# Ones behind the second mixer's values, and five short stretches in another order, in a two-block transformer on one core

## What is computed

```
x = x + gt1 * merge(attention(h), gla(h));  x = x + gt2 * square(relu(h2 @ w1)) @ w2     # first block
h = h + mlstm(rmsnorm(h))                                                                # second mixer
h = h + square(relu(rmsnorm(h) @ w1)) @ w2
h = h + sigmoid(rmsnorm(h) @ gate_w + b) * (p @ ple_w)
return rmsnorm(h) * norm_final
```

```
num = s @ v            # 256 values a head
den = sum of s over the keys
h   = num / max(abs(den), exp(-m))
```

## Time and profile before

| | us |
|---|---|
| median of 3 runs | 924.65 (924.34 to 925.21) |
| profiled execution | 924.22 |
| its span | 922.4 |
| PE busy | 896.7 (97%) |
| PE weight loads busy | 766.2 (83%) |
| DVE busy | 624.5 (68%) |
| ACT busy | 478.7 (52%) |
| POOL busy | 10.0 (1%) |

### The profile page before, as it was taken

The page is one execution under the profiler, slowest core; times in us unless marked ns, Lnnn a source line. Parts: engine busy times, 40 slices in busy tenths (PEclk is TensorE's granted clock), DMA queues, the critical chain, the costliest instruction groups (busy, mean ns, idle before and its releaser), DMA issues.

```text
span 922.4 us, 14154 instructions
## 1 busy us (share of the span) xinstructions
PE 896.7 (97%) x5144; PEld 766.2 (83%) x5144; DVE 624.5 (68%) x990; ACT 478.7 (52%) x759; POOL 10.0 (1%) x21
## 2 busy tenths in 40 slices
PE   7999999999999999999999999999999999999995
PEld 2788888887788887889999998897888999999984
DVE  2668779879688878765555557766767855555577
ACT  3647545565565575465444444444645744444453
POOL 0200000000000000000000000000000000000000
PEclk9999999999999999999999999999999999999998
DMA  9955212326346877646555558254334665555521
GB/s 360 340 180 178 70 52 86 114 92 200 114 143 227 255 245 246 218 141 210 183 183 182 182 185 270 94 183 141 131 114 159 224 223 198 196 191 193 188 91 46
DMA packets 45376, 162.10 MB, mean 176 GB/s; under 512 B 5616, under 2 KB 5760, under 8 KB 45329
## 3 DMA queue, kind: packets, MB, share of 16 engines
q1 hardware_dynamic: 42896, 155.73, 50.0%
q0 software_dynamic: 1296, 4.02, 1.6%
q10 hardware_dynamic: 1136, 1.70, 0.5%
HBM read 160.39 MB, written 1.05 MB: 175 GB/s over the span
## 4 chain that ended last, share of the span: by engine, by line
PE 82%; DVE 9%; ACT 4%; DMA 3%; issue 2%; SPq 0%; DVEq 0%; ACTq 0%
PE bank L685 68%; DVE w_lo L1657 3%; DMA arena<-in_early 2%; PE bank L857 2%; PE bank L940 1%; PE bank L1137 1%; ACT w_hi L1233 1%; PE bank L847 1%; DMA raw<-in_stream 1%; PE bank L960 1%; PE bank L955 1%; PE bank L1166 1%; PE bank L864 1%; PE bank L805 1%; DVE act_lo L1657 1%
## 5 line engine op out<-in xcount | busy, mean ns | idle before, releaser
L1657 DVE TENSOR_TENSOR w_lo<-raw,w_hi 128x1024 fp32r<-128x1024 f32 x244 | 288.1, 1220 | 161.8 <-ACT w_hi L1233 161.5
L1233 ACT ACTIVATE w_hi<-raw 128x1024 fp32r<-128x1024 f32 x244 | 245.0, 1051 | 195.1 <-PE bank L685 165.4
L685 PE MATMUL bank<-w_hi,act_lo 128*128 128x512 f32 x720 | 293.0, 407 | 0.1
L685 PE MATMUL bank<-w_lo,act_hi 128*128 128x512 f32 x720 | 281.3, 391 | 0.0
L685 PE MATMUL bank<-w_hi,act_hi 128*128 128x512 f32 x720 | 280.8, 390 | 0.0
L685 PE MATMUL bank<-act_lo,w_hi 128*128 128x256 f32 x640 | 183.0, 286 | 3.6 <-DVE act_lo L1657 2.5
L685 PE MATMUL bank<-act_hi,w_hi 128*128 128x256 f32 x640 | 181.1, 283 | 0.0
L685 PE MATMUL bank<-act_hi,w_lo 128*128 128x256 f32 x640 | 181.0, 283 | 0.0
L685 PEld LDWEIGHTS bank<-w_lo,act_hi 128*128 128x128 f32 x720 | 135.1, 188 | 29.3
L685 PEld LDWEIGHTS bank<-w_hi,act_lo 128*128 128x128 f32 x720 | 135.5, 188 | 26.7 <-issue 1.7
L685 PEld LDWEIGHTS bank<-w_hi,act_hi 128*128 128x128 f32 x720 | 135.6, 188 | 26.2 <-issue 1.4
(11 more groups left out here) (250 smaller groups left out, 782.9 us busy)
## 6 DMA issues: line engine op xcount, KB each, us to landing
raw<-in_stream SPq DMA_DIRECT2D x278, 512.0 KB, 4.5
arena<-in_early SPq DMA_DIRECT2D x14, 512.0 KB, 12.0
res<-in_x ACTq DMA_DIRECT2D x1, 1024.0 KB, 8.9
raw<-in_early SPq DMA_DIRECT2D x2, 512.0 KB, 13.6
arena<-in_ctx SPq DMA_DIRECT2D x1, 1024.0 KB, 13.5
res<-in_x POOLq DMA_DIRECT2D x1, 1024.0 KB, 7.7
arena<-in_norm_final POOLq DMA_DIRECT2D x1, 512.0 KB, 4.4
arena<-in_ple_b POOLq DMA_DIRECT2D x1, 512.0 KB, 5.4
```

What stands on the lines that cost most here:

```text
L685: last = pe.matmul(o, left, right, start=start and m == 0, stop=stop and m == 2, skip_group_check=shared)
L1233: return act.activation(o, i, ACT.Copy)
L1657: return dve.tensor_tensor(o, x, hi.bitcast(F32), ALU.subtract)
```

## The change

Five places are altered. First, the values `mv` get a 257th column per head that holds ones (set by one memset on DVE), so that each numerator of the first token block also yields its sum as the 257th column. A bank has 512 columns, so for the second token block columns 128 to 255 with the ones go into banks 6 and 7 (129 columns) and columns 0 to 127 into bank 4 (128 columns). DVE reads the sums in two instructions and divides in three pieces a direction. `mv`, `mo` and `m_d` are laid out anew in the same buffers.

Second, in attention, ("qkturn", 1) stands ahead of item 1, and ACT moves the transposed probabilities out before the exponential of the same step. Third, for n2 DVE scales quarters of 512 columns, PE transposes blocks 0 and 1, does the product `pw` that stood behind all four, and then blocks 2 and 3. Fourth, at n3 DVE leaves cuts 2 and 3 of `mq` until the residual is done, and takes the turn of blocks 0 and 1 ahead of the third piece. Fifth, in the tail the multiplications by the last gain go: one into a fused instruction per token block (res * scale * gain), one to POOL for token block 0; the evacuation of the third piece stands ahead of the chain for token block 0, and its multiplication and addition behind it.

```diff
-    p.woven("go0", [None, att[0], None, att[1], ("qkturn", 1)] + att[2:6], ada=7)
+    p.woven("go0", [None, att[0], ("qkturn", 1), att[1], None] + att[2:6], ada=7)
...
-    p = Plan(p_cuts("mq") + [last(0, 0), last(0, 1), last(1, 0), ("turn", "n3", (0, 1)), last(1, 1)])
+    p = Plan([("round", "mq", 0), ("cut", "mq", 0), ("round", "mq", 1), ("cut", "mq", 1), ("round", "mq", 2),
+              ("round", "mq", 3), last(0, 0), last(0, 1), last(1, 0), ("turn", "n3", (0, 1)), ("added", "a", 1, 0),
+              last(1, 1), ("cut", "mq", 2), ("cut", "mq", 3)])
...
-                ("mm", "pg1", 0, 2), ("mm", "pg1", 0, 3), ("evac", "pg1", 0), ("square", 1), ("rows_out", 0)])
-    for n in ("pg0", "pg1"):
-        p.steps += p.group(n, 1) + [("evac", n, 1), ("square", 2 + int(n[2]))]
-    p.steps.append(("rows_out", 1))
+                ("mm", "pg1", 0, 2), ("mm", "pg1", 0, 3), ("evac", "pg1", 0), ("square", 1)])
+    p.steps += p.group("pg0", 1) + [("evac", "pg0", 1), ("final", 0), ("gated", 2), ("square", 2)]
+    p.steps += p.group("pg1", 1) + [("evac", "pg1", 1), ("square", 3), ("final", 1)]
...
-        mv = tiles2(2)
-        mo = tiles2(4)
-        m_d = slots(6)[:, 0:768].rearrange("p (j n) -> p j n", j=2)
+        mv_at, mo_at, md_at = 0, TT * GH * (DV + 1), TT * GH * (DV + 1) + TT * D
+        mv = slots(2, 5)[:, mv_at:mo_at].rearrange("p (t h e) -> p t h e", t=TT, h=GH)
+        mo = slots(2, 5)[:, mo_at:md_at].rearrange("p (t n) -> p t n", t=TT)
+        m_d = slots(2, 5)[:, md_at:md_at + 768].rearrange("p (j n) -> p j n", j=2)
...
+            pool.wait_ge(late_in, 32)
+            pool.wait_ge(res_ready, RES_AT["out"] + 2)
+            pool.tensor_tensor(x_out[:, 0, NC:D], res[:, 0, NC:D], fin_row[:, NC:D], ALU.mult).then_inc(x_gained, 1)
...
-                    elif b < TT:
-                        pe.wait_ge(norm_ready, TT * i + t + 1)
+                    elif b < TT or name == "n2":
+                        pe.wait_ge(norm_ready, TT * i + b + 1)
...
-                    turn(name)
+                    turn(name, (0, 1))
                     mm("pw", 3, 0)
+                    turn(name, (2, 3))
...
+                    if h == 0:
+                        pe.wait_ge(ones_set, 1)
                     for (d, t), parts in terms.items():
+                        c0, o = (0, 0) if t == 0 else (P, DV + 1)
                         for n, (j, c) in enumerate(parts):
-                            pe.matmul(psum[6 + d][:, t * DV:(t + 1) * DV], m_s[:, j, c:c + P],
-                                      mv[:, j, h * DV:(h + 1) * DV], start=(n == 0), stop=(n == len(parts) - 1))
+                            pe.matmul(psum[6 + d][:, o:o + DV + 1 - c0], m_s[:, j, c:c + P], mv[:, j, h, c0:DV + 1],
+                                      start=(n == 0), stop=(n == len(parts) - 1))
                     heads = sum(s[:2] == ("mhead", "a") for s in PLAN2[:PLAN2.index(("mhead", part, h))])
                     pe.wait_ge(mh_arg, heads)
                     for (d, t), parts in terms.items():
+                        if t == 0:
+                            continue
                         for n, (j, c) in enumerate(parts):
-                            last = pe.matmul(psum[4][:, 2 * t + d:2 * t + d + 1], m_s[:, j, c:c + P], ones[:, 0:1],
+                            last = pe.matmul(psum[4][:, d * P:(d + 1) * P], m_s[:, j, c:c + P], mv[:, j, h, 0:P],
                                              start=(n == 0), stop=(n == len(parts) - 1))
                     last.then_inc(mh_num, 1)
...
+                    if n[:2] == "mv":
+                        h = 2 * int(n[2])
+                        o, i = mv[:, which, h:h + 2, 0:DV], bank[:, :].rearrange("p (h e) -> p h e", h=2)
...
+                if t == 0:
+                    act.wait_ge(x_gained, 1)
...
             def attention(i):
-                if i < N_ATT:
-                    act.wait_ge(nmax_ready, i + 1)
-                    if i >= 3:
-                        act.wait_ge(pt_done, i - 2)
-                    at = (i % TT) * QH + i // TT
-                    act.activation(prob[:, i % 3, :], psum[4 + i % 2][:, :], ACT.Exp, bias=stat[:, 0, i:i + 1],
-                                   scale=q_scale[:, 0, at:at + 1], accum_out=stat[:, 1, i:i + 1]).then_inc(exp_done, 1)
                 j = i - 3
...
                                    ACT.Copy).then_inc(pt_evac, 1)
+                if i < N_ATT:
+                    act.wait_ge(nmax_ready, i + 1)
+                    if i >= 3:
+                        act.wait_ge(pt_done, i - 2)
+                    at = (i % TT) * QH + i // TT
+                    act.activation(prob[:, i % 3, :], psum[4 + i % 2][:, :], ACT.Exp, bias=stat[:, 0, i:i + 1],
...
+                if name == "n2":
+                    for b in range(TT):
+                        norm_quarter(b)
+                    return
...
+            def norm_quarter(b):
+
+                t, half = b % TT, slice(b // TT * NC, (b // TT + 1) * NC)
...
+                    if name == "n2" and b == 0:
+                        norm_quarter(2)
+                        norm_quarter(3)
...
+                    if i != 2:
+                        gated(i)
+
+            def gated(i):
...
-            def final_scale(i):
-
-                t, j = OUT_PIECES[i]
-                half = slice(j * NC, (j + 1) * NC)
-                if i == 0:
-                    dve.wait_ge(late_in, 32)
-                dve.wait_ge(res_ready, RES_AT["out"] + i + len(OUT_HALVES[i]))
-                ins = dve.tensor_tensor(x_out[:, t, half], res[:, t, half], fin_row[:, half], ALU.mult)
-                if j == 0:
-                    return
-                chain(ins)
+            def final_scale(t):
+
+                i = 2 * t + 1
+                if t == 1:
+                    dve.wait_ge(res_ready, RES_AT["out"] + i + len(OUT_HALVES[i]))
+                    chain(dve.tensor_tensor(x_out[:, t, NC:D], res[:, t, NC:D], fin_row[:, NC:D], ALU.mult))
...
-                dve.tensor_scalar(x_out[:, t, 0:NC], x_out[:, t, 0:NC], y, None, ALU.mult).then_inc(out_dve, 1)
+                dve.scalar_tensor_tensor(out=x_out[:, t, 0:NC], in0=res[:, t, 0:NC], scalar=y, in1=fin_row[:, 0:NC],
+                                         op0=ALU.mult, op1=ALU.mult).then_inc(out_dve, 1)
...
+                dve.memset(mv[:, :, :, DV:DV + 1], 1.0).then_inc(ones_set, 1)
...
-                    chain(dve.tensor_scalar(den.bitcast(I32), psum[4][:, 0:4].bitcast(I32), NO_SIGN, None,
-                                            ALU.bitwise_and))
                     den_v = den.rearrange("p (t d) -> p t d", t=2)
+                    for d in range(2):
+                        sums = psum[6 + d][:, DV:DV + P + 2:P + 1]
+                        ins = dve.tensor_scalar(den_v[:, :, d].bitcast(I32), sums.bitcast(I32), NO_SIGN, None,
+                                                ALU.bitwise_and)
+                    chain(ins)
                     chain(dve.tensor_tensor(den_v, den_v, mg_e[:, :, :, h], ALU.max))
                     chain(dve.reciprocal(den, den))
-                    for t in range(TT):
-                        s = slice(t * DV, (t + 1) * DV)
-                        ins = dve.tensor_scalar(m_h[:, t, h * DV:(h + 1) * DV], psum[6][:, s],
+                    spans = lambda d: ((0, 0, DV, psum[6 + d], 0), (1, 0, P, psum[4], d * P),
+                                       (1, P, DV, psum[6 + d], DV + 1))
+                    for t, lo, hi, bank, c in spans(0):
+                        ins = dve.tensor_scalar(m_h[:, t, h * DV + lo:h * DV + hi], bank[:, c:c + hi - lo],
                                                 stat[:, 0, 2 * t:2 * t + 1], None, ALU.mult)
                     chain(ins)
-                    for t in range(TT):
-                        o = m_h[:, t, h * DV:(h + 1) * DV]
-                        s = slice(t * DV, (t + 1) * DV)
-                        ins = dve.scalar_tensor_tensor(out=o, in0=psum[7][:, s], scalar=stat[:, 0, 2 * t + 1:2 * t + 2],
-                                                       in1=o, op0=ALU.mult, op1=ALU.add)
+                    for t, lo, hi, bank, c in spans(1):
+                        o = m_h[:, t, h * DV + lo:h * DV + hi]
+                        ins = dve.scalar_tensor_tensor(out=o, in0=bank[:, c:c + hi - lo],
+                                                       scalar=stat[:, 0, 2 * t + 1:2 * t + 2], in1=o, op0=ALU.mult,
+                                                       op1=ALU.add)
...
-                elif kind == "last":
+                elif kind == "added" or kind == "last" and step[1:] != ("a", 1, 0):
```

31 lines of the change are left out of this document (20 added, 11 removed).

## The result

The changed kernel takes 916.15 us (median of 4 runs, 915.5 to 916.87) against 924.93 us (4 runs): a ratio of 0.9905, with a 95% interval of 0.9891 to 0.9919. 916.4 was forecast. The profiled execution took 916.24 with a span of 914.3, against 924.22 and 922.4: 8.0 us less of span, where the sum said 8.2. By the medians it is 8.8.

The account below looks back on a forecast made before the run. PE was taken to bound the kernel, busy 896.7 of 922.4 us. The terms 4.1 + 1.1 + 0.5 + 0.6 + 1.9 = 8.2 gave 916.0, or 916.4 as a median; range of 8 in 10: 914.6 to 919.6.

Parts of the forecast that it names:

- the sum: All five parts' terms together: 8.2 us less than the kernel before.
- Ones: Second mixer's heads: ones as a 257th column shorten PE's products by 1.22 us a head; 4.1 us net gain.
- The payment by DVE: Second mixer's heads: DVE's extra sum read and division pieces cost PE 0.8 us, 0.6 of it in head 0.
- the forecast sign: Second mixer: PE's wait before the spread of the second head's gates grows from 0.2 to about 0.8 us.
- The half-rate rival: Second mixer's heads: products of 257 and 128 or 129 columns stream at half rate, giving 926.8 us; chance 0.03.
- Attention: Attention's first items: of 1.8 us of PE idle time in three waits, 1.1 us is gained.
- The bound of 1.06: Attention's third wait: DVE was idle only 1.06 us there, so work can come at most that much earlier.
- n2: At n2: DVE's scaling in smaller pieces lets PE's block 1 start sooner; 0.5 us gained.
- n3: At n3: products start 1.3 us earlier, about 0.7 is given back at mq's third unit; 0.6 us gained.
- Tail: Behind PE's last matmul: the last evacuation no longer waits for DVE and the rest is as before; 1.9 us gained.
- POOL's operation: Tail: POOL's multiplication of 512 costs nothing up to 2.9 us; contention with DVE might lower the sum by 0.1.
- the 2.9 of cover: Tail: POOL's multiplication starts at about 905.7 and ACT wants it at about 908.6, so 2.9 us are free.

Follow-up runs that it names:

- e_act: The kernel before with only ACT's order in attention altered (probabilities moved out before the exponential): 922.52 us against 924.35, ratio 0.9978.
- f_head: The changed kernel with the second head's scores multiplied by DVE ahead of the cut that stood before them: 915.71 us.
- f_lo: The changed kernel with DVE's low part of the second pair of attention outputs taken ahead of the maximum of item 4: 915.29 us.
- f_pool: The changed kernel with POOL also multiplying the second token block's first half by the last gain: 915.41 us.
- e_norms: The kernel before with only the new orders at n2 and n3: 924.25 us against 924.26, ratio 1.0001.
- f_best: The changed kernel with the edits of f_lo, f_head and f_pool, and cut 2 of mq ahead of n3's turn: 913.90 us.
- f_nopool: The changed kernel with POOL's multiplication done by DVE ahead of the first token block's chain: 915.88 us, ratio 0.9905.

## Why the prediction was right, term by term

- **Ones, 4.1 forecast, 4.27 measured** (4.32 alone). A head's products fell by 1.29 rather than 1.22, 5.2 for four: the twelve instructions of 128 or 129 columns were priced at 0.111, and took that but for the last, 0.03. The payment by DVE was charged at 0.8, 0.6 of it for head 0. PE's lead fell by 0.44 at the third head's gates and by 0.42 behind the last head, where PE waits for DVE's cut. On DVE the stretch from the sums to the next scores (L2208 to L2200) took 0.32 longer, 5.88 instead of 5.56, where 0.6 was worked out. That head 0 had no slack was true, but not for the reason given: the 0.2 ahead of L1120 is the second head's gates at 624.94, ahead of head 0's products, and there the changed kernel doesn't wait at all. The wait that the forecast sign meant stands at the third head's gates, and is 0.53 where 0.8 was expected. The half-rate rival is refuted by the single starts.
- **Attention, 1.1 forecast, 1.47 measured.** The mechanism (ACT's order lets go, DVE's full row takes over) was right. The bound of 1.06 came from two gaps on DVE in 2 us, counted from the recorded end of one operation to the start of the next. An operation that doesn't wait starts 0.08 or 0.09 ahead of the recorded end of the one before (in the changed kernel the products of 1.53 from 229.59 end at 231.12, and the next operation starts at 231.04). From start to start the two gaps were 0.52 and 0.70: 1.22. By the third output 1.24 were gained, and 0.23 more by 261 us, which I hadn't looked at. Wrong was the share of the moved query transposes: I took their 0.58 as gone, and e_act shows that the edit brought nothing of it.
- **n2, 0.5 forecast, 0.50 measured** in the changed kernel, 0.45 and 0.49 in f_head and f_lo, 0.30 in f_pool, 0.02 in e_norms, and a loss in f_best. Half of it came at the first wait (0.71 to 0.44) and half at the second (1.20 to 0.93), where the prediction put all of it at the second. What it left out is the transfer that the norm's sums hang on behind ACT's queue; that this is what takes n2's gain away is read from the waits, not shown.
- **n3, 0.6 forecast, 0.58 measured.** Both halves, the 1.3 won at the first product and what is given back at the third unit, came as worked out.
- **Tail, 1.9 forecast, 1.46 measured.** The evacuation came 1.92 earlier against PE, as forecast. The mis-sized step is the end: I wrote that from there it is as before, and left out that the fused operation, priced at 0.26 more for the first token block, is the last thing that DVE does for the second. It takes away the stagger of the two stores. f_pool restores it and gets 1.93.
- **POOL's operation.** It took 1.29, within the 2.9 of cover. DVE's first small operation of the chain took 0.52, not 0.16, and ended as POOL's did (900.41 beside 900.39); in f_nopool it took 0.16, with POOL idle. All eight traces with this operation on POOL show 0.51 to 0.54. By the Trainium skill, page "SBUF — State Buffer", section "Who interferes with whom", a DVE instruction with two inputs in SBUF contends with a GpSimd instruction that reads SBUF. The trace agrees: the hold was 0.36, and slack covered it. In f_pool a DVE multiplication started 0.14 ahead of the recorded end of POOL's second operation and was no longer than its like (0.42), so there the overlap left no mark. The prediction's remark that POOL has no work beside DVE is true of arithmetic alone: in the kernel before it issued transfers beside DVE, from 39.44 on.

That the sum hit within 0.3 us is in part luck: attention's and the heads' terms were 0.5 too low together, the tail's 0.4 too high, and the changed kernel's trace lost 0.28 in its first 45 us. It stays open why e_norms' last store landed 0.89 late, and whether it did so in its other ten runs.

## What to carry to other kernels

Where two engines wait for each other within a microsecond, a removed wait is worth only the gap on the engine behind it: add up that engine's gaps from start to start, and expect the rest as a new wait with a new name. A column of ones beside real columns is nearly free, while a matmul of one column costs as much as one of 128. In the last microseconds count the operation on each queue that stores: here two stores that started together ended 0.3 to 0.4 us later than two that were 0.24 apart.
